# Both down products as seven block products, with weight sums made in DRAM

## What is computed

```python
# first block
h = rms_norm(x, norm_ffn_pre)
f = (silu(h @ w_gate) * (h @ w_up)) @ w_down          # (512, 2816) @ (2816, 1024)
x = x + rms_norm(f, norm_ffn_post)
# second block
h2 = rmsnorm(x, norm2_g)
x = x + (silu(h2 @ w_gate_2) * (h2 @ w_up_2)) @ w_down_2
return rmsnorm(x, final_g)
```

## Time and profile before

| | |
|---|---|
| median of three runs | 1117.66 us (1117.46 to 1119.12) |
| span of the profiled execution, first to last instruction | 1115.9 us |
| what lies around the span, to the median | 1.8 us |
| TensorE / VectorE / ScalarE / GpSimd busy | 98% / 75% / 55% / 11% of the span |
| DMA | 109.3 MB in all, 98 GB/s on the mean |
| TensorE's granted clock | 0.997 of full speed |

### The profile page before, as it was taken

One profiled execution on the slowest core, in us unless ns is written; L12 is line 12 of the kernel. 1 busy time (PEld: TensorE's weight loads), 2 busy tenths in 40 slices (PEclk: granted clock), 3 DMA queues, 4 the chain that ended last, 5 costly groups with the idle time before them and its releaser, 6 DMA issues.

```text
span 1115.9 us, 18197 instructions
## 1 busy us (share of the span) xinstructions
PE 1092.9 (98%) x6848; PEld 972.0 (87%) x6848; DVE 832.3 (75%) x1425; ACT 612.6 (55%) x1109; POOL 121.2 (11%) x143
## 2 busy tenths in 40 slices
PE   9999989999999999999999999999999999999997
PEld 6788877899999999888898887787899999988886
DVE  6898886798989888833378878566699898884333
ACT  6787785486555555522255558545555555563231
POOL 1476744000000000000000004200000000000000
PEclk9999999999999999999999999999999999999999
DMA  7323312312332333333313320031233233333312
GB/s 282 126 59 93 88 49 96 113 65 87 115 98 95 113 114 112 125 105 113 110 70 115 93 81 17 20 103 65 79 114 114 97 95 113 114 132 114 95 57 76
DMA packets 34150, 109.30 MB, mean 98 GB/s; under 512 B 4368, under 2 KB 7056, under 8 KB 33936
## 3 DMA queue, kind: packets, MB, share of 16 engines
q1 hardware_dynamic: 33312, 107.22, 29.5%
q10 hardware_dynamic: 752, 0.92, 0.3%
HBM read 100.78 MB, written 2.10 MB: 92 GB/s over the span
## 4 chain that ended last, share of the span: by engine, by line
PE 89%; DVE 5%; ACT 3%; issue 1%; DMA 1%; POOL 1%; ACTq 0%; SPq 0%; DVEq 0%
PE bank L551 13%; PE bank L553 13%; PE bank L552 13%; PE bank L2145 11%; PE bank L2144 11%; PE bank L2143 11%; PE bank L1086 2%; PE bank L1076 2%; PE bank L1031 1%; PE bank L1032 1%; PE bank L1033 1%; PE bank L1159 1%; PE bank L1160 1%; PE bank L1161 1%; PE bank L2630 1%
## 5 line engine op out<-in xcount | busy, mean ns | idle before, releaser
L472 DVE TENSOR_TENSOR wl<-raw,wh 128x1024 fp32r<-128x1024 f32 x108 | 134.0, 1242 | 132.0 <-ACT wh L460 131.6
L460 ACT ACTIVATE wh<-raw 128x1024 fp32r<-128x1024 f32 (+1 forms) x109 | 114.0, 1049 | 163.7 <-PE bank L553 152.8
L2143 PE MATMUL bank<-h,wh 128*128 128x256 f32 x576 | 163.0, 283 | 0.0
L2144 PE MATMUL bank<-h,wh 128*128 128x256 f32 x576 | 163.0, 283 | 0.0
L2145 PE MATMUL bank<-h,wl 128*128 128x256 f32 x576 | 163.0, 283 | 0.0
L2145 PE MATMUL bank<-hh,wl 128*128 128x256 f32 x432 | 122.3, 283 | 0.0
L2144 PE MATMUL bank<-hl,wh 128*128 128x256 f32 x432 | 122.3, 283 | 0.0
L2143 PE MATMUL bank<-hh,wh 128*128 128x256 f32 x432 | 122.2, 283 | 0.0
L551 PE MATMUL bank<-gh,wh 128*128 128x512 f32 x308 | 119.8, 389 | 0.0
L552 PE MATMUL bank<-gl,wh 128*128 128x512 f32 x308 | 119.8, 389 | 0.0
L553 PE MATMUL bank<-gh,wl 128*128 128x512 f32 x308 | 119.8, 389 | 0.0
(11 more groups left out here) (309 smaller groups left out, 2652.6 us busy)
## 6 DMA issues: line engine op xcount, KB each, us to landing
raw<-weights SPq DMA_DIRECT2D x181, 512.0 KB, 3.6
xres<-x_t SPq DMA_DIRECT2D x8, 512.0 KB, 6.2
sw<-ta SPq DMA_DIRECT2D x36, 64.0 KB, 2.0
out_t<-final SPq DMA_DIRECT2D x6, 256.0 KB, 2.1
q<-sw SPq DMA_DIRECT2D x10, 128.0 KB, 2.3
q<-ta SPq DMA_DIRECT2D x10, 128.0 KB, 2.3
rope<-angles SPq DMA_DIRECT2D x1, 1024.0 KB, 10.3
sw<-ta ACTq DMA_DIRECT2D x4, 64.0 KB, 2.8
```

The lines of the kernel that those rows point to most:

```text
L460: act.activation(wh[:, j, :, n], raw[:, j, :, n], ACT.Copy).then_inc(high_split, 1)
L472: v.tensor_tensor(wl[:, j, :, :], raw[:, j, :, :], wh[:, j, :, :].bitcast(F32), ALU.subtract)\
L2143: pe.matmul(o, wh_half[:, h, k, :], high[:, k, :], start=first and k == 0, stop=False, skip_group_check=True)
L2144: pe.matmul(o, wh_half[:, h, k, :], low[:, k, :], start=False, stop=False, skip_group_check=True)
```

## The change

Both down products are written as two by two blocks: the hidden layer in two halves of 11 tiles, the output features in two halves of 512 columns, the tokens in two halves of 256. Seven products (`SEVEN`, in the order P1, P2, P6, P5, P7, P3, P4) take the place of eight. Each has 11 tiles x 2 blocks of 128 tokens x 3 parts = 66 matmuls. Tokens are now stationary and 512 columns of weights move, so the result has tokens on partitions.

- Weights: a chunk now is two rows of tiles by 512 columns (`PER` = 6 chunks a product, the last a half one). P1, P2 and P4 read stored blocks; P6, P5, P7 and P3 read sums of blocks, which eight transfers in DRAM make for each down product: four copies and four transfers that add, one behind the other (`gpsimd_weight_sums`). SyncE waits for the sum that a chunk belongs to.
- Tokens: GpSimd makes the sums of blocks of the hidden layer (`gpsimd_token_sums`), ScalarE and VectorE split the operand of each product in three pieces (`act_token_high`, `vec_token_low`), where before every hidden tile was split once.
- Results: ScalarE takes products out of PSUM and VectorE adds (`act_take`, `vec_join`). Sums of squares are ScalarE's `accum_out`, so the products with the matrix of ones go. In the first block the scaled rows are turned back by TensorE, 32 transposes of 128 x 128 (`pe_turn_rows`), half of them in the down product and half in the next projection. In the second block x is turned, also with 32 transposes (`pe_turn_x`), and the result is stored by token rows; its last quarter comes last (`first_block`).
- `pe_factor` brings the token factor of the norm before into a column, by four matmuls of one column.

```diff
-DOWN = (8, 8, 6)
+PAIR_TILES = FT // 2
+BATCHES = (slice(0, 4), slice(4, 8), slice(8, PAIR_TILES))
+PER = (PAIR_TILES + 1) // 2
...
+SEVEN = (P1, P2, P6, P5, P7, P3, P4)
+BASE = {P1: W11, P2: W12, P4: W22}
+SUMMED = {P5: S1, P6: S2, P7: S3, P3: S4}
...
+        STEPS_SUMMED = {S1: 2, S2: 4, S4: 6, S3: 8}
+
+        def gpsimd_weight_sums(g, dn):
+
+            s = [dn.sums[i].rearrange("c p k n -> (c p) (k n)") for i in range(4)]
+            row = 4 * KB
+            g.dma_start(s[S1], blocks(dn, W21), max_dma_last_dim=row).then_inc(dn.sums_made, 16)
+            g.wait_ge(dn.sums_made, 16)
+            g.dma_start(s[S1], blocks(dn, W22), accum_op=ALU.add, max_dma_last_dim=row).then_inc(dn.sums_made, 16)
+            g.wait_ge(dn.sums_made, 32)
...
+            g.dma_start(s[S3], blocks(dn, W21), accum_op=ALU.add, max_dma_last_dim=row).then_inc(dn.sums_made, 16)
+            g.wait_ge(dn.sums_made, 128)
...
+        def gpsimd_token_sums(g, dn):
...
+            for batch in BATCHES:
+                t = ktiles(0, batch)
+                hidden_made(g, gu, t.stop - 1)
+                g.tensor_tensor(gwhole[:, t, early], gwhole[:, t, late], gwhole[:, t, early], ALU.subtract).then_inc(sums.of, 1)
+            reached(g, gu.product, 2 * GROUPS)
...
+        def pe_block(pe, dn, x, chunk, row, b):
+
+            p, k, slot = SEVEN[x], 2 * chunk + row, (dn.c0 + PER * x + chunk) % RING
+            bank, n = down_pair(p)[b], slice(b * P, (b + 1) * P)
+            high, low = high_tokens[x % 2][:, k, n], low_tokens[x % 2][:, k, n]
+            pe.matmul(bank[:, :], high, wh_row[:, slot, row, :], start=k == 0 and p in (P1, P2, P5), stop=False, skip_group_check=True)
+            pe.matmul(bank[:, :], high, wl_row[:, slot, row, :], start=False, stop=False, skip_group_check=True)
+            return pe.matmul(bank[:, :], low, wh_row[:, slot, row, :], start=False, stop=k == PAIR_TILES - 1, skip_group_check=True)
...
+        def pe_down1(pe):
+
+            for x in range(7):
+                chain_free(pe, down1, SEVEN[x])
+                if x == 1:
+                    pe_factor(pe, down1)
+                for chunk in range(PER):
+                    if x == 6 and chunk == 3:
+                        pe_turn_rows(pe, 0, (0, 1))
+                    if x == 6 and chunk == 4:
+                        pe_turn_rows(pe, 0, (2, 3))
+                    pe_chunk(pe, down1, x, chunk)
...
+        def vec_down_step(v, dn, x):
+
+            for n in range(PER if x < 6 else 2):
+                vec_split(v, dn.c0 + PER * x + RING + n)
+                if x < 6 and n < len(BATCHES):
+                    vec_token_low(v, dn, x + 1, n)
...
+        def act_down1(act):
+
+            i0 = CHUNK0["in2"]
...
+            act_row_scale(act, 0)
+            act_scale_rows(act, 0)
+            act_down_step(act, down1, 6, 0)
+            act_down_step(act, down1, 6, 1)
+            act_split(act, i0)
+            for b in (2, 3):
+                act_row_square(act, down1, b, 0, rows_of(b, 0))
+            for k in (0, 1):
+                act_half_h(act, join2, k, 0)
+            act_split(act, i0 + 1)
+            for k in (2, 3, 4):
+                act_half_h(act, join2, k, 0)
+            act_split(act, i0 + 2)
+            for k in (5, 6, 7):
+                act_half_h(act, join2, k, 0)
+            act.wait_ge(used, multiplied(down1, 7, 0))
+            for b in (2, 3):
+                act_row_square(act, down1, b, 1, as_rows(PAIR_B[b - 2][:, :]))
+            act_split(act, i0 + 3)
+            act_row_scale(act, 1)
+            act_scale_rows(act, 1)
...
+                    p = SEVEN[x]
+                    if p in BASE:
+                        source = w_in[STORED0[name] + PER * BASE[p] + i]
+                    else:
+                        sp.wait_ge(downs[name].sums_made, 16 * STEPS_SUMMED[SUMMED[p]])
+                        source = downs[name].sums[SUMMED[p], i]
...
             for t in range(TICK0, TICKS):
                 gpsimd_tick(g, t)
+            gpsimd_weight_sums(g, down1)
+            gpsimd_token_sums(g, down1)
+            gpsimd_weight_sums(g, down2)
             gpsimd_attention2(g)
+            gpsimd_token_sums(g, down2)
```

More of the change, by code:

```diff
@@ new lines, in chunk_rows, with pe_chunk_ready, pe_chunk @@
+        def chunk_rows(chunk):
+            return range(1 if chunk == PER - 1 else 2)
+        def pe_chunk_ready(pe, dn, x, chunk):
+            slot_wait(pe, dn.c0 + PER * x + chunk)
+            if chunk % 2 == 0:
+                reached(pe, dn.token_low, len(BATCHES) * x + chunk // 2 + 1)
+        def pe_chunk(pe, dn, x, chunk):
+            pe_chunk_ready(pe, dn, x, chunk)
+            for row in chunk_rows(chunk):
+                for b in range(2):
+                    ins = pe_block(pe, dn, x, chunk, row, b)
+            ins.then_inc(used, 1)
@@ new lines, in pe_factor, with row_bank @@
+        def pe_factor(pe, dn):
+            for b in range(QB):
+                ins = pe.matmul(banks[5][:, b:b + 1], rstd[:, b * P:(b + 1) * P], ident[:, 0:1], start=True, stop=True)
+            ins.then_inc(dn.factor_turned.of, 1)
+        rows_scaled_v = sem("down1_rows_scaled_v")
+        rows_scaled_a = sem("down1_rows_scaled_a")
+        rows_turned = sem("down1_rows_turned")
+        def row_bank(half, group):
+            return ((banks[4], banks[5], banks[3], banks[4]), (banks[5], banks[4], banks[6], banks[7]))[half][group]
@@ L2950 @@
     put("norm2", _per_feature(a["norm2_g_2"][0]))
-    put("final", _per_feature(a["final_g_2"]))
     put("eps", _np.full((P, 1), EPS, f))
```

766 lines of the change are left out of this document (462 added, 304 removed).

## The result

The changed kernel takes 1157.07 us (median of 4 runs, 1156.94 to 1162.1), the kernel before 1117.85 in the same series: ratio 1.0361, 95% interval [1.0341, 1.0381], 39 us slower. Forecast were 1106.8 us and a range of 1091 to 1140.

What follows compares the result with a forecast made beforehand. TensorE, working 98% of the span, was taken as the bound. Matmuls 34.2 + 0.3 less, transposes and factor 8.4 + 1.2 more, end 2 less, handover 3 more: 23.9 us less; transfers 13 more: 1106.8 us, range 1091 to 1140.

Steps and rivals of the forecast that it cites:

- What goes, and the pitch: Down products: 462 matmuls each stay at the old pitch of 0.2267 us; 17.1 us drop from each, 34.2 us together.
- The end: After the last matmul's start: one 128x512 quarter left, 6.0 us instead of 8.2, so 2 us less.
- Handing over: Passage to the second block: TensorE's transposes of late tokens wait for their rows, 3 us once (0 to 8).
- Token sums on GpSimd ... Free: Down product: nine GpSimd passes take 19 to 29 us, are done before they are wanted, and cost nothing.
- The first eight steps cost nothing: DRAM transfers from 181.1 us: even at the highest price they end at 450 us, wanted by 452.
- The second eight at 13 us: DRAM transfers beside the first down product: they delay weight loads by 13 us, between 8 (low) and 26 (middle).
- rival B: Adding transfers take two passes: 26 us lost in the first down product, 1119.8 us, no measurable change; chance 0.17.
- The sign that the prediction named: SyncE's landing time of weight chunks rises from 3.6 to over 6 us only while the DRAM steps run.
- Rival C: Transfers pay reads and writes: TensorE waits 66 us in down product, 30 at attention; 1190 us, half price 1155; chance 0.20.
- TensorE without waits: TensorE runs without waits up to about 476 us; waits in the gate and up stages would show the forecast wrong.
- the base: Whole kernel with the transfers costing nothing: 23.9 us less, 1093.8 us.
- Rival D: Ring of weight chunks too short even alone: each of 14 products loses 1.3 us, 18 together, 1112 us; chance 0.08.

Runs made afterwards that it cites:

- neither: Changed kernel without the sixteen DRAM steps and with the twelve token-sum instructions shrunk to 2 elements each, so no sums are computed: 1104.14 us, ratio 0.9868.
- small_token_sums: Changed kernel with GpSimd's twelve token-sum instructions shrunk to 2 elements each, token sums not computed: 1129.09 us, ratio 1.0093.
- vector_sums_second_late: Changed kernel with token sums on VectorE and the second eight DRAM steps begun only with the second block's projections: 1118.49 us, ratio 1.0000.

## Why the prediction was wrong

- **What goes, and the pitch**: right. With neither the first down product takes 107.5 us to the next stage's first start (107 forecast).
- **The end**: nearly right. From the last matmul's start (1148.8) to the span's end are 6.6 us where 8.3 stood; 6.0 forecast.
- **Handing over**: right in size. From the last products to gate/up of the second block 4.8 us more in neither than before (239.4 against 234.6), 3 of waits and 2 of transposes forecast. The wait for the scaled late rows is 2.5 us.
- **"Token sums on GpSimd ... Free"** is the step that failed first. They were in time, and their 26.6 us lie in the forecast's 19 to 29, in part by luck: by themselves, at the 2.4 and 1.86 us that such passes take in the gate/up stage, nine would be 20 us; each engine seems to hold the other up. What the prediction left out is what they do to the engine beside them: it priced VectorE's splits at 1.24 us throughout, and beside GpSimd they took 3.12. 20 us in the two down products, and some 8 shared with the steps: 28. The Trainium skill has the rule that the prediction did not weigh: by "GPSIMD Engine Reference", section Specifications, GpSimd's way into SBUF is shared with VectorE and contends with VectorE's instructions that read two SBUF inputs. The splits (raw and wh) are such; the trace agrees, 1.22 against 3.12 us.
- **"The first eight steps cost nothing"** failed. The argument asked only whether they end in time. They end at 339, but from 266 on they run beside the gate/up stage and cost it 5 us, 12 with the token passes behind them.
- **The second eight at 13 us**: mis-sized, 20.1 measured in the first down product (small_token_sums), between the forecast's value and rival B's 26. A step takes longer than one pass of data at 345 GB/s (9.1 us) by far: about 16 for a copy, 25 for an add. The Trainium skill, "Collectives: The Full Stack", section on the bandwidth ceiling, has the adds of a reduce-scatter at half the rate of copies; here an add takes 1.6 times as long as a copy on the mean, so the rule is near and the measurement decides. The sign that the prediction named came true: chunks of 512 KB landed after 8.6 to 9.3 us on the median while steps ran, and after 3.6 to 3.9 beside the second down product. Rival C's second place, attention waiting for the eighth step, did not occur in the changed kernel, only in vector_sums_second_late. That C's 1155 us at half its price lies near 1157 is luck: it puts the whole loss on the transfers, which alone cost 25 us, and the kernel is slower although no pair of steps passed the 50 us that C asked for.
- **"TensorE without waits" in gate/up**, called the base's weak point by the forecast itself, failed by 4 us in each of the two stages (neither); what takes them is read from the trace, not shown. Rival D, the ring too short alone, is refuted: without both suspects the waits for weight splits in 14 products are 0.7 us.

The sum by measured terms: 1118 before; 14 less for the base (1104.1); 25 for the steps alone, 19 for GpSimd's sums alone, 9 for what they do to each other: 1157. Held against the forecast of 1106.8: 10 us are the base, 12 the transfers, 28 the token sums on GpSimd with what they share with the transfers.

## What to carry to other kernels

Work put on an idle engine is not free because that engine is idle: ask what its busy neighbour will slow to, and try the busy neighbour itself if it has gaps. A background transfer is priced by the stage beside it, not by its deadline; put it beside a stage with thin loads, off the queue of an engine that the path waits for, and give it smaller rows than the transfers that must win. Where two causes overlap, take them away one by one and both together, since the shared part belongs to neither.

## What the runs showed of the hardware

- GpSimd's and VectorE's elementwise work of two SBUF operands do not run side by side at full speed: 128x1024 on VectorE 1.22 us alone, 3.12 beside GpSimd's, whose own passes of that size took 2.4 us apart in gate/up and 2.9 to 3.2 in the down product. Smaller VectorE instructions were held up as long: 128x512 from 0.69 to 2.88 us, 128x768 from 0.95 to 3.12.
- DRAM to DRAM beside loads, 3.15 MB in 4 KB rows: a copy 13 to 19 us, an add 23 to 28; in 1 KB rows beside the loads of a down product 19 and 39 us.
- Where the DMA engines are full, the row size of the background transfers changed what the foreground got: 127.8 and 109.0 us for the same down product at 4 KB and 1 KB.
- The granted clock falls after short stalls of TensorE: 2.4 us without work, then 0.66 for four us. The longest 512-column matmuls took 0.79 us instead of 0.39. No experiment separated what that costs from the waits; by busy time it is at most 18 of 54 us.
- Left open: whether VectorE's instructions with one SBUF input are slowed as well (not tried), and why a copy in DRAM takes 15 us when the same engines moved over 300 GB/s at other times.
